# Two layers of conv and sparse attention, then a gated block: borders reordered, conv tiles spread over the attention

## The reference

```python
for l in range(DEPTH):                       # DEPTH = 2
    a, g, zc, q, k, v, za, qi, ki, wi = split(h @ w_in[l])
    u = conv31(a * sigmoid(g)) + b           # causal, 31 taps, one filter a channel
    y_conv = silu(layer_norm(u)) * silu(zc)
    y_attn = sparse_attention(rope(q), rope(k), v, top 132 of the index scores) * silu(za)
    h = layer_norm(ALPHA * h + [y_conv, y_attn] @ w_out[l])
# the second block, on the 512 rows
q, k, v, gate_a, u, v_in, gate_b, g_merge = split(rmsnorm(h) @ w_in_2)
y_a = (block_attention(rope(rmsnorm(q)), rope(rmsnorm(k)), v) * silu(gate_a)) @ w_a
y_b = (gelu(u) * mix(layernorm(gelu(v_in))) * silu(gate_b)) @ w_b
h = h + (g[0] * y_a + g[1] * y_b) @ w_out_2
return rmsnorm(h)
```

## Time and profile before

| | |
|---|---|
| median of 3 runs | 1048.1 us (1047.66 to 1052.39) |
| the profiled execution: time | 1051.77 us |
| its span, first to last instruction | 1050.0 us |
| mean granted clock of TensorE, share of full | 0.986 |
| PE busy | 996.0 us, 95% |
| DVE, ACT, POOL busy | 652.2, 581.5, 197.6 us |

### The profile page before, as it was taken

How to read it: one execution, slowest core, us unless ns; L and a number is a source line. 1 busy time by engine, 2 the same in 40 slices (tenths; PEclk the granted TensorE clock), 3 DMA queues, 4 the chain that set the end, 5 groups by cost and what they waited for, 6 DMA issues and landing times.

```text
span 1050.0 us, 16512 instructions
## 1 busy us (share of the span) xinstructions
PE 996.0 (95%) x6452; PEld 842.3 (80%) x6452; DVE 652.2 (62%) x1423; ACT 581.5 (55%) x944; POOL 197.6 (19%) x238
## 2 busy tenths in 40 slices
PE   6999999998999899999999899789999899999997
PEld 6998988885677899898888677678888778887885
DVE  3899999876673389899986555627522333332522
ACT  6585891657444458588265834534656565554331
POOL 0100671013111110077011312232200000000001
PEclk9999999999999999999999899989999999999999
DMA  7775884744203667487383611865778535466651
GB/s 288 179 189 163 216 183 125 182 100 121 41 1 115 167 168 180 118 195 172 115 201 81 180 35 41 234 147 150 186 182 218 120 87 133 109 145 136 165 155 81
DMA packets 23820, 152.35 MB, mean 145 GB/s; under 512 B 2864, under 2 KB 3376, under 8 KB 6848
## 3 DMA queue, kind: packets, MB, share of 16 engines
q0 software_dynamic: 9648, 68.75, 35.2%
q1 hardware_dynamic: 14096, 82.55, 21.9%
HBM read 149.20 MB, written 2.10 MB: 144 GB/s over the span
## 4 chain that ended last, share of the span: by engine, by line
PE 80%; ACT 10%; DVE 4%; DMA 3%; issue 2%; POOL 0%; POOLq 0%; SPq 0%; DVEq 0%; ACTq 0%
PE psum_B L1257 20%; PE psum_A L1257 15%; PE psum_A L1290 9%; PE psum_B L1290 9%; PE psum_A L1439 5%; PE psum_C L1332 2%; DMA w_lo<-in_weights 2%; PE psum_A L1651 2%; PE psum_B L1439 2%; ACT w_hi L632 2%; PE psum_B L1651 2%; ACT w_lo L633 2%; PE psum_B L1393 2%; ACT exps L753 1%; PE psum_D L1257 1%
## 5 line engine op out<-in xcount | busy, mean ns | idle before, releaser
L1735 DVE SCALAR_TENSOR_TENSOR conv_acc<-u,vec,conv_acc 128x528 f32<-128x528 f32 (+1 forms) x240 | 172.3, 754 | 3.2
L1061 POOL DMA_DIRECT2D w_lo<-in_weights x67 | 59.3, 886 | 588.0 <-ACT w_lo L633 561.8
L1257 PE MATMUL psum_B<-x_hi,w_hi 128*128 128x264 f32 (+3 forms) x480 | 134.8, 321 | 5.2 <-DVE mlp_lo L2189 3.6
L632 ACT ACTIVATE w_hi<-w_raw 128x2048 fp32r<-128x2048 f32 (+2 forms) x85 | 129.5, 1523 | 12.2 <-DMA w_raw<-in_weights 11.6
L1257 PE MATMUL psum_B<-x_lo,w_hi 128*128 128x264 f32 (+3 forms) x480 | 132.6, 317 | 0.0
L1257 PE MATMUL psum_B<-x_hi,w_lo 128*128 128x264 f32 (+3 forms) x480 | 132.1, 316 | 0.0
L633 ACT ACTIVATE w_lo<-w_raw 128x2048 fp32r<-128x2048 f32 (+2 forms) x85 | 128.8, 1515 | 0.0
L1257 PE MATMUL psum_A<-x_hi,w_hi 128*128 128x264 f32 (+2 forms) x528 | 125.4, 291 | 2.2 <-DVE za L1882 1.2
L1257 PE MATMUL psum_A<-x_lo,w_hi 128*128 128x264 f32 (+2 forms) x528 | 122.7, 287 | 0.0
L1257 PE MATMUL psum_A<-x_hi,w_lo 128*128 128x264 f32 (+2 forms) x528 | 122.7, 287 | 0.0
L1257 PEld LDWEIGHTS psum_A<-x_hi,w_hi 128*128 128x128 f32 x528 | 87.5, 188 | 6.4 <-issue 3.0
(11 more groups left out here) (349 smaller groups left out, 2123.3 us busy)
## 6 DMA issues: line engine op xcount, KB each, us to landing
w_raw<-in_weights SPq DMA_DIRECT2D x67, 1024.0 KB, 5.3
w_lo<-in_weights POOLq DMA_DIRECT2D x65, 1024.0 KB, 8.5
x_first<-in_x_t SPq DMA_DIRECT2D x4, 528.0 KB, 6.9
h<-in_x SPq DMA_DIRECT2D x1, 2048.0 KB, 11.0
out<-h SPq DMA_DIRECT2D x4, 512.0 KB, 2.6
post_ln_g<-in_post_ln_g SPq DMA_DIRECT2D x2, 512.0 KB, 9.5
post_ln_b<-in_post_ln_b SPq DMA_DIRECT2D x2, 512.0 KB, 10.5
w_raw<-in_weights SPq DMA_DIRECT2D x2, 288.0 KB, 5.3
```

Source lines behind the costliest of these rows:

```text
L632: act.activation(whi[n % RING][:, a:b], raw[n % RING][:, a:b], ACT.Copy)
L1061: pool.dma_start(wlo[n % RING][:, 0:width], io["weights"][n, :, 0:width], accum_op=ALU.add) \
L1257: mm = pe.matmul(ps[0:cols, i, 0:b - a], w[wp][:, kt, at:at + cols], x[xp][:, kt, a:b], start=(kt == 0 and wp + xp == 0), stop=(kt == KD - ...
L1735: got = dve.scalar_tensor_tensor(dst, src, w, dst, ALU.mult, ALU.add)
```

## The change

The order of uses at a border changes (attention half (0, 4) ahead of (1, 3)); rows of kv and q are interleaved; conv tiles 2 to 4 get later items, their forth turns all into bank D; the conv half of tile 4's projection goes two items sooner, its second column half into bank C; splits of the first three blocks after a border are written out by hand, the first in halves on either side of the last y high part; turned x goes to banks given by a table; the mix constants are loaded after the raw block of vin.

```diff
+KV_AND_Q = (("kv", 0), ("kv", 1), ("kv", 2), ("q", 0), ("kv", 3), ("q", 1), ("q", 2), ("q", 3))
...
-        uses.extend([(l, "wo", 0, 4, "conv"), (l, "wo", 1, 4, "conv"), (l, "wo", 1, 3, "conv"), (l, "wo", 1, 3),
-                     (l, "wo", 0, 4), (l, "wo", 1, 4)])
+        uses.extend([(l, "wo", 0, 4, "conv"), (l, "wo", 1, 4, "conv"), (l, "wo", 1, 3, "conv"), (l, "wo", 0, 4),
+                     (l, "wo", 1, 3), (l, "wo", 1, 4)])
...
 CONV_AT = {
-    0: ((0, 8, "D", "C"), (1, 10, "B", "C"), (2, 12, "D", "C"), (3, 14, "B", "C"), (4, 16, "D", "C")),
-    1: ((1, 8, "D", "C"), (2, 10, "B", "C"), (3, 12, "D", "C"), (4, 14, "B", "C")),
+    0: ((0, 8, "D", "C"), (1, 10, "B", "C"), (2, 14, "D", "C"), (3, 18, "D", "C"), (4, 22, "D", "C")),
+    1: ((1, 8, "D", "C"), (2, 10, "B", "C"), (3, 14, "D", "C"), (4, 18, "D", "C")),
 }
...
-OUTPUT_CONV_AT = {0: 39, 1: 31}
-OUTPUT_BANK = ("A", "B")
+OUTPUT_CONV_AT = {0: (37, 39), 1: (29, 31)}
+OUTPUT_BANK = (("A", 1), ("C", 0))
+INPUT_BANK = {0: ("D", "B", "D", "D", "C"), 1: (None, "D", "B", "D", "C")}
...
-                if key == (2, "q", 1):
+                if key == (2, "vin", 0):
                     load_mix()
...
+                after = NUMBER[(l + 1, "a" if l < DEPTH - 1 else "kv", 0)]
+                split_hi(after, 0)
                 y_hi(l, "attn", 4)
-
-                next_blocks((l, "wo", 1, 4, "conv"))
+                split_hi(after, 1)
                 if l < DEPTH - 1:
                     x_hi(l, 0)
-                    x_hi(l, 1)
-                    next_blocks((l, "wo", 1, 3))
-                    for t in (2, 3, 4):
-                        x_hi(l, t)
-                    next_blocks((l, "wo", 1, 4))
+                x_hi(l, 1)
+                x_hi(l, 2)
+                split_hi(after + 1)
+                if l < DEPTH - 1:
+                    x_hi(l, 3)
+                    x_hi(l, 4)
+                    split_hi(after + 2)
                 else:
-                    x_hi(l, 1)
-                    x_hi(l, 2)
                     squares(3, square)
-                    next_blocks((l, "wo", 1, 3))
-                    x_hi(l, 3)
-                    squares(4, square)
-                    next_blocks((l, "wo", 1, 4))
-                    x_hi(l, 4)
+                    split_hi(after + 2)
...
-            for name in ("kv", "q"):
-                for t in range(4):
-                    take_rows(name, t)
+            for name, t in KV_AND_Q:
+                take_rows(name, t)
+                if (name, t) == ("kv", 1):
+                    x_hi(DEPTH - 1, 3)
+                    squares(4, square)
+                elif (name, t) == ("kv", 2):
+                    x_hi(DEPTH - 1, 4)
+                    split_hi(NUMBER[(2, "vin", 0)])
+                elif name == "q":
+                    next_blocks((2, "q", t))
...
                 part_low(l, "attn", 4)
-                next_blocks((l, "wo", 1, 4, "conv"))
-                ln_deviation((l, "post", 3), 3, P)
-                if l == DEPTH - 1:
+                after = NUMBER[(l + 1, "a" if l < DEPTH - 1 else "kv", 0)]
+                split_lo(after)
+                if l < DEPTH - 1:
+                    ln_deviation((l, "post", 3), 3, P)
+                    split_lo(after + 1)
+                    ln_deviation((l, "post", 4), 4, P)
+                    split_lo(after + 2)
+                else:
+                    ln_deviation((l, "post", 3), 3, P)
+                    split_lo(after + 1)
                     input_deviation(3)
-                next_blocks((l, "wo", 1, 3))
-                ln_deviation((l, "post", 4), 4, P)
-                if l == DEPTH - 1:
+                    split_lo(after + 2)
+                    ln_deviation((l, "post", 4), 4, P)
                     input_deviation(4)
-                next_blocks((l, "wo", 1, 4))
...
+            split_lo(NUMBER[(2, "vin", 0)])
             for t in range(4):
-                next_blocks((2, "kv", t))
                 unit_scale("k", t)
+            next_blocks((2, "q", 1))
...
                 turn["AB"] = 1
-                output_conv(l, 1)
-                if l == DEPTH - 1:
-                    turn_rows(l, 1)
-                output_rows(l, 1, 3, "A", 0)
+                ps = claim((l, "wo", 1, 3), "A", (0,))[:, 0, :]
+                output_half(l, 1, 0, 3, ps).then_inc(psum_full.mark((l, "wo", 1, 3, "conv")), 1)
                 if l < DEPTH - 1:
                     turn_rows(l, 0)
-                    turn_rows(l, 1)
+                turn_rows(l, 1)
                 output_attn(l, 0)
                 turn_rows(l, 2)
+                output_half(l, 1, 1, 3, ps).then_inc(psum_full.mark((l, "wo", 1, 3)), 1)
                 output_attn(l, 1)
...
+            for name, t in KV_AND_Q:
+                if name == "kv":
+                    x_ready(1, t + 1)
+                    rows((2, "kv", t), NUMBER[(2, "kv", 0)], x, META + P * t, 1, 2 * P, 0, KD)
+                    if t in (1, 2):
+                        turn_rows(1, t + 2)
+                else:
+                    rows((2, "q", t), NUMBER[(2, "q", 0)], x, META + P * t, 2)
...
                 if l < DEPTH - 1:
-                    residual(l, 1, 3)
-                    aggregate(l, 3)
                     x_lo(l, 0)
                     x_lo(l, 1)
...
+                residual(l, 0, 4)
+                x_lo(l, 2)
+                residual(l, 1, 3)
+                aggregate(l, 3)
+                post_norm(l, 3)
+                residual(l, 1, 4)
+                if l == DEPTH - 1:
                     second_input(3)
-                    residual(l, 1, 4)
-                    aggregate(l, 4)
-                    post_norm(l, 4)
-                    x_lo(l, 3)
+                aggregate(l, 4)
+                post_norm(l, 4)
+                x_lo(l, 3)
+                if l == DEPTH - 1:
                     second_input(4)
                 x_lo(l, 4)
```

More of the change, by code:

```diff
@@ L145, in weight_stream @@
     blocks.append(((l, "kv", 0), BLOCK, (l, "kv", 3)))
-    uses.extend((l, "kv", t) for t in range(4))
-    halves(l, "q", range(4))
+    for half in range(2):
+        blocks.append(((l, "q", half), BLOCK, (l, "q", 3)))
+    uses.extend((l, *row) for row in KV_AND_Q)
     for name in ("vin", "u", "gb"):
@@ L289, in attention_extras @@
             todo["pool"][i + 1].append(("input", t))
-    todo["pe"][OUTPUT_CONV_AT[l]].append(("wo conv", 0))
+    for part, i in enumerate(OUTPUT_CONV_AT[l]):
+        todo["pe"][i].append(("wo conv", part))
     if l == 0:
@@ L946, in take_rows @@
                     act.activation(sgb[t][:, :], ps[:, 0, :], ACT.Silu).then_inc(act_took.mark(use), 1)
-                next_blocks(use)
             def take_gates(name, c):
@@ L1015, in _ @@
                     take_rows(name, t)
+                    next_blocks((2, name, t))
                     if name == "u":
@@ L1417, in turn_rows @@
                 use = (l, "xT", t)
-                ps = claim(use, next_buf("CD"))
+                ps = claim(use, INPUT_BANK[l][t])
                 n = SIZE[t]
@@ L1445, in output_rows @@
                 ps = claim(use, buf, (bank_,))[:, 0, :]
-                mm = output_half(l, n, 0, t, ps)
-                if (n, t) == (1, 3):
-                    mm.then_inc(psum_full.mark((l, "wo", 1, 3, "conv")), 1)
+                output_half(l, n, 0, t, ps)
                 output_half(l, n, 1, t, ps).then_inc(psum_full.mark(use), 1)
             def output_conv(l, n):
-                ps = claim((l, "wo", n, 4), OUTPUT_BANK[n], (1,))[:, 0, :]
+                buf, at = OUTPUT_BANK[n]
+                ps = claim((l, "wo", n, 4), buf, (at,))[:, 0, :]
                 output_half(l, n, 0, 4, ps).then_inc(psum_full.mark((l, "wo", n, 4, "conv")), 1)
             def output_attn(l, n):
-                output_half(l, n, 1, 4, bank[OUTPUT_BANK[n]][:, 1, :]).then_inc(psum_full.mark((l, "wo", n, 4)), 1)
+                buf, at = OUTPUT_BANK[n]
+                output_half(l, n, 1, 4, bank[buf][:, at, :]).then_inc(psum_full.mark((l, "wo", n, 4)), 1)
             def x_ready(l, t):
@@ L1497, in _ @@
                         use = (l, name, c)
-                        ps = claim(use, next_buf("AB" if turned else "CD"))
+                        ps = claim(use, next_buf("AB") if turned else "D")
                         w, cols, at = channel_weights(l, name, c)
@@ L1653, in branch @@
                 mm.then_inc(psum_full.mark(use), 1)
-            for t in range(4):
-                x_ready(1, t + 1)
-                rows((2, "kv", t), NUMBER[(2, "kv", 0)], x, META + P * t, 1, 2 * P, 0, KD)
-                if t < 2:
-                    turn_rows(1, t + 3)
-            for t in range(4):
-                rows((2, "q", t), NUMBER[(2, "q", 0)], x, META + P * t, 2)
+            for name, t in KV_AND_Q:
[6 more added lines that the diff above has]
+                    rows((2, "q", t), NUMBER[(2, "q", 0)], x, META + P * t, 2)
             for name in ("vin", "u", "gb"):
@@ L2048, in _ @@
```

(9 more changed lines are left out.)

1 line of the change is left out of this document (removed).

## The result

| | before | after |
|---|---|---|
| median | 1047.88 us (4 runs, 1045.80 to 1052.39) | 1060.32 us (4 runs, 1057.33 to 1062.11) |
| profiled execution: time, span | 1051.77, 1050.0 us | 1061.84, 1060.0 us |
| granted clock, mean over the span | 0.986 | 0.979 |

The ratio of the runs is 1.0101, with a 95% interval of 1.0068 to 1.0134: slower by some 10.6 us (the two medians are 12.4 apart). The forecast was 1049.5 in a range of 1040 to 1056, and 0.17 for slower. Ratios are of undisturbed runs; a single run of 2451.87 us in a later experiment (POOL's order changed) is left out.

What follows compares the result with a forecast made beforehand. PE, busy 95% of the span, was taken as the bound, so gains could come only from its idle time or low clock. Terms +2.7 + 1.7 + 3.6 - 0.3 - 6.3 = +1.4 us gave 1049.5 us, range 1040 to 1056.

Steps and rivals of the forecast that it cites:

- Layer 0, "+2.7 us": Layer 0's attention: item 22 comes 1.2 us sooner, but the projection of item 25 starts at 278.3 instead of 275.57.
- The queue at item 23: Layer 0: DVE does y, statistics, meta rows' residual and two masked logits in turn, to 276.9; logits 28 wait for it.
- The claim that the stops up to item 17 stay: Layer 0: tile 2 takes tile 3's old places, so PE's stops up to item 17 and their low-clock window remain.
- One more such stretch, +1.7 us: Layer 0: stops of 1.2 and 2.3 us bring one more low-clock stretch on PE, +1.7 us, or 0 without it.
- Layer 1, "+3.6 us": Layer 1's attention: tile 4's back turn and logits 26 wait over bank C; next projection at 623.7 instead of 620.13.
- The claim of bank A, "+0.65 us": Each border: tile 4's conv-half projection, two items sooner, claims bank A and waits for tile 3's residual, +0.65 us.
- First border, "-0.3 us": Border to layer 1: g block's load goes out at about 345.3; taking 10 us, it gives -0.3 us.
- rival C: Border to layer 1: shared DMA engines make the g block's load take 12.89 us; total 1052.5, chance 0.13.
- the +2.7 that stood as the upper end: Border to layer 1: +2.7 us if the g block's load takes 12.89 us.
- Border to the second block, "-6.3 us": Second block: kv rows 2 wait for tile 3's x until 678.9, yet vin starts at 709.5 against 715.78.
- Rival A: Faster: bank C is free soon and item 23 takes no longer, so the conv tiles pay; -9.7, 1038.4, chance 0.22.
- Rival B: Slower: the chain into kv rows 2 runs late and the second border's 6.3 us are lost; +7.7, 1055.8, chance 0.15.

Runs made afterwards that it cites:

- the borders alone: The changed kernel with the old conv table, so only the two borders differ from the kernel before; median 1047.41 us, ratio 0.9977.
- the second of the two with only layer 1's table changed: Kernel before with layer 1's conv tile 3 at item 14 and tile 4 at item 16 in bank B; median 1051.03 us, ratio 1.0016.
- the fastest version: Changed kernel, old conv table, g block's low-part load ahead of tile 3's deviation, tile 4's conv-half product one item later; median 1043.86 us, ratio 0.9950.
- experiment 2, first run: Changed kernel with layer 0's loads of post norm gain and bias held until wo(1,1)'s low parts landed; median 1058.97 us, ratio 1.0078.

## Why the prediction was wrong, point by point

- **Layer 0, "+2.7 us", is the step that failed first.** It went from item 22 coming 1.2 us sooner straight to DVE's queue, and never asked when the meta product's weights land. Before, PE had paused there for 0.11 us, at 269.26: the load was just in time. A kernel that brings PE there 0.6 us sooner, and the load 1.4 us later, stops for 2.1. With the load out 3.0 us sooner the stop is gone and the projection of item 27 starts 4.6 us sooner in the trace; the times of the runs are too near each other to show it. The queue at item 23 itself was right: the stops of 1.2 and 2.3 us came as 0.50 and 2.21, only 3.3 us late as a whole, to the end of y. The claim that the stops up to item 17 stay was loose as well: two of 1.05 and 1.55 us came as 1.80 and 0.80.
- **"One more such stretch, +1.7 us"** at half clock: the second failed step: the term was mis-sized. I counted the clock in layer 0 alone and for one pair of stops. In the profiled executions it costs up to 7.2 us more than before (5.3 by PE's busy time). Whether the stretch at 241 to 252 is the change's isn't shown: it has 3.9 against 1.5, but in the profiles of all kernels it costs 2.5 to 4.0 us with layer 0's new places (six profiles) and 0 to 4.5 with the old ones (eight). The three behind the change's own stops are 1.7, 2.7 and 1.7; at the second border two of 1.7 replace 1.7 and 2.8.
- **Layer 1, "+3.6 us"**: right in place and size. The back turn stood 1.66 us for neg_max (forecast 1.7) and logits 26 1.80 (1.8); the profile puts the latter down to DVE h, which ended at 632.37, but ACT's affine out of bank C, the forecast's releaser, ended at 632.44, and the logits began at 632.54. From the projection of item 17 (601.52 against 590.93) to that of item 23 (633.63 against 620.13) PE fell back by 2.9; the half clock behind it, 1.7 more, is what I left out.
- **The claim of bank A, "+0.65 us"**: 1.51 against the 0.88 that it replaces, 0.63 at each border.
- **First border, "-0.3 us"**: the third failed step, rival C. In the borders alone the issue was right to 0.2 us, the load's duration was not: 12.7 us, not 10. The first block's load took 12.7 as well, whose cost the sum had at nothing, and g starts 2.35 us late, near the +2.7 that stood as the upper end. (In that profile 1.5 of it is back by the next group, because no half clock follows.) In the change itself g's load took 11.64 us and the stage cost 1.8.
- **Border to the second block, "-6.3 us"**: right in size. -5.6 in the change, though partly by luck: there PE's own turn came late, and ACT's high part behind it set kv rows 2, 0.8 us after DVE's norm was done; and -7.8 in the borders alone, by the very chain that was worked out (678.47 against 678.9).
- Rival A fell: bank C was not free. Rival B fell: the border kept its gain. The range's upper end, 1056, had no case in which several stops each bring their half clock, nor one of a stop at the meta product.

## What to carry to other kernels

Moving work in a tightly woven stage moves every load that the stage only just met; look for waits of a tenth of a microsecond before the change, since they mark what will stop next. A new stop of 2 us costs 2 us and, in some of the executions here, another 1.5 to 2.7 at half clock behind it; stops of 2.67 and 3.10 us in the borders alone had none. And before an operation is placed, list who holds its bank at that item: three of the placements tried here lost to a bank that was still held, and what an experiment moved to avoid one holder it put behind another.

## What the runs showed that I had not expected

- The same code gets the half clock or not. Up to 252 us the kernel before, the second of the two with only layer 1's table changed, the borders alone and the fastest version have the same order of work, and their granted clocks from 241 to 252 us are 0.84, 0.53, 0.69 and 1.00. First that window of the kernel before with layer 1's tile 4 at item 16 in bank B, then that of the fastest version (columns as above):

```profile
241.00:252.00 11.00, 9.82 (x33) 5.17 (x34) 7.86 (x23) 7.45 (x16) 4.52 (x7) 0.53 0.80 213
```

```profile
241.00:252.00 11.00, 7.81 (x48) 4.16 (x48) 7.85 (x23) 7.73 (x19) 4.20 (x7) 1.00 0.82 223
```

  The Trainium skill (TensorE: Matmul & The Clock Gate, The HAM clock gate) says of a kernel's start that the activity window behind the clock is free-running and that how many matmuls run slow varies from run to run. These rows, from the middle of a kernel, agree with that, 0.53 against 1.00. A profiled execution is thus one draw: the borders alone were 8.3 us shorter than before in the two profiled spans, and 2.4 us by all runs.
- A low-part load of 1 MB took 8.0 to 13.1 us. The long ones have raw loads beside them, 10.6 with one and 12.7 with two at the first border, but the fastest version had 10.1 and 11.3 with its raw loads sent off in the same order. Among loads of wo(1,1), 8.0 (the kernel before) and 8.9 (experiment 2, first run) have no other load beside them, and nothing in the trace tells why they differ.
